# Row-wise weight stages, norm sums inside them, normed rows in PSUM and a later reload of x in a two-block transformer kernel

## The chip, the cores and the metric

The kernel runs on one core of one Trainium2 chip. The metric is the device time of one execution in microseconds (us); the kernel before was timed in three runs.

## What is computed

512 tokens of width 1024 pass through two blocks. In the parts that matter here:

```python
# first block
x = x + gate1 * mixed                      # mixed = (gated branches) @ w_out
h2 = rms_norm(x, g_norm2) * (1 + scale2) + shift2
x = x + gate2 * peer_ffn(h2, w_peer_q, ...)   # top 16 of 128 x 128 experts, 8 heads
# second block, i = 0: windowed attention, i = 1: latent attention
u = rms_norm_2(h, norm_g[i])
y = (attention(u) * silu(z)) @ w_out
h = h + y
gate = sigmoid(rms_norm_2(h, ple_norm_g[i]) @ ple_w_gate[i])
h = h + (p[i] @ ple_w[i]) * gate
# after both
return rms_norm_2(h, final_norm_g)
```

## The kernel before

It is written engine by engine, with its own semaphores; each engine's order is the order of the code. Activations lie transposed: `xT` (the residual) and `hT` (the normed rows) have 8 rows of 128 features by 512 tokens. Every fp32 weight and activation is cut into a high and a low fp16 part, and a product is three fp16 matmuls (`three`, L624). Weights come as tiles of 128x1024 through a ring of four in SBUF (SP, L465); POOL cuts each into parts (L573, L574, L576), also a ring of four: for tile n it waits until PE has begun tile n-3 (semaphore `begun`).

**Stages.** `features` computes one output of 128 features by 512 tokens after another: output m takes the 8 rows k in order, 24 matmuls, and one weight tile. Banks 0 to 3 of PSUM hold the sums in turn; output m waits until output m-4 was taken (`need_bank`), and in output 0 each row k waits for its input (`need(k)`). `ple_w0` and `ple_w1` have two rows, so 6 matmuls an output. `tokens` is the other form: four sums side by side, row by row.

**Norms.** Seven norms (n = 0 to 6) go alike. ACT squares the 8 rows of `xT` into `hT` (L985), PE sums them with a matrix of ones (`norm_part`, L672, an fp32 matmul that the trace shows as two), ACT takes the root (L987), DVE the reciprocal (L1187). Then for each row DVE multiplies (L1190) into `whole`, two rows in SBUF, ACT copies the high part to `hT` (L980, L997), DVE subtracts to get the low part (L1198, L1200) and signals `h_ready`. Stages behind norms: `peer_q` (norm 1), `a_q` (2), `ple_g0` (3), the tokens stage `b_c` (4), `ple_g1` (5); norm 6 gives the output.

**Attention outputs.** PE turns eight blocks into banks 4 to 7; DVE multiplies each with its gate into `whole` (L1578) and cuts it (L1218, L1219); `a_out` and `b_out` read the result. DVE adds their sums to `xT` (L1425).

**Gates.** ACT writes the sigmoid of each `ple_g` output to SBUF (L1133), DVE multiplies (L1594) and adds to `xT` (L1596).

**Experts.** 128 chunks go up (24 matmuls each, into PSUM banks 0 and 1 in turn; ACT's gelu at L1064; SP stores the result, L514); 64 of them have gate matmuls beside them. Four stores of 8 MB take the gates to `gate_mem` (L1095). `xT` was parked in memory before, since its place holds the gates' working rows; it is read back at L1097, right behind the last of these stores on ACT's queue. 64 gates are done by chunk 112; 16 chunks of gelu follow. DVE needs `xT` again at the end of the down phase. Places of the old program that the steps use:

```python
act.dma_start(gate_mem[...], spread[...])            # L1095, four times
act.dma_start(xT[:, :, :], x_park...)                # L1097
gelus(AT_GATES + S // GROUP, CHUNKS)                 # the last 16 chunks
...
norm(1); features("peer_q", hr, h_need(1))           # PE
features("a_out", ...); features("ple_w0", ...)
norm(3); features("ple_g0", hr, h_need(3)); norm(4)
```

## Time and profile before

| | |
|---|---|
| median of 3 runs | 2800.81 us (2798.86 to 2802.94) |
| the profiled execution's own time | 2798.45 us |
| its span | 2796.6 us |
| busy: PE, DVE, ACT, POOL | 2515.2, 1558.5, 594.7, 1602.1 us |
| mean granted TensorE clock | 0.953 of 2.4 GHz |

Busy times are those of instructions; matmuls overlap, so a stage's length is read from starts and from who takes its sums. In a timeline row stand the start and length in us, the engine, line, operation, the tiles, how many instructions, and in brackets the idle time before it with the engine whose work ended it. "ACTq" and "SPq" are DMA issues. Runs of the same kind are merged into one row, whose length reaches from the first start to the last end.

### The profile page before, as it was taken

Reading aid. Unit: us, or ns where it says so; the run is one execution under the profiler, and the core shown is the slowest. Engines: PE = TensorE matmul, PEld = TensorE weight load, DVE = VectorE, ACT = ScalarE, POOL = GpSimd, SP = SyncE. Lnnn points to the kernel's source line nnn. Section 1 sums busy time; section 2 is a strip of 40 time slices with the busy share of each in tenths; the row PEclk is TensorE's granted clock in tenths of the full one; section 3 lists DMA queues with packets and bytes.
Section 4 is the critical chain, followed back from the end, with each engine's and each line's share of the span. In section 5 each row is a group of like instructions: output and inputs, shape, how many; then the busy total and the mean of one; then the engine's idle time right before and its main releaser. Section 6 shows DMA issues by size and latency. Waiting matters only on the chain.

```text
span 2796.6 us, 38708 instructions
## 1 busy us (share of the span) xinstructions
PE 2515.2 (90%) x12856; PEld 1260.3 (45%) x12856; DVE 1558.5 (56%) x2823; ACT 594.7 (21%) x1243; POOL 1602.1 (57%) x1048
## 2 busy tenths in 40 slices
PE   3767788999999999978999999999898888989987
PEld 1423443444455555433444444444355533557633
DVE  6498583699967777505952222250218836555525
ACT  1111221111122222201111111110125322245412
POOL 4535435799976767659976666660560157830053
PEclk7878898999999999989999999999999999999998
DMA  6216312354446587577765555560220022310021
GB/s 228 98 44 215 118 38 80 113 150 143 146 147 199 179 249 246 166 217 254 261 220 204 201 204 201 204 224 15 84 83 1 9 75 68 106 53 1 9 75 38
DMA packets 189252, 375.45 MB, mean 134 GB/s; under 512 B 13536, under 2 KB 79200, under 8 KB 189152
## 3 DMA queue, kind: packets, MB, share of 16 engines
q1 hardware_dynamic: 119696, 332.64, 35.8%
q10 hardware_dynamic: 69456, 41.49, 5.0%
q8 instruction: 61, 1.00, 0.1%
q14 instruction: 39, 0.32, 0.0%
HBM read 302.77 MB, written 71.30 MB: 134 GB/s over the span
## 4 chain that ended last, share of the span: by engine, by line
PE 77%; DVE 12%; DMA 3%; issue 2%; ACT 2%; POOL 2%; ACTq 1%; SPq 0%; DVEq 0%; POOLq 0%
PE ps L624 65%; PE ps L714 3%; PE ps L734 3%; PE ps L840 2%; PE ps L723 2%; DMA arena<-ada_w 2%; DVE arena L1280 2%; PE ps L672 1%; ACTq L1097 1%; DVE arena L1384 1%; DVE arena L1383 1%; DVE spare L1190 1%; DVE arena L1245 1%; ACT arena L1016 1%; DVE arena L1218 1%
## 5 line engine op out<-in xcount | busy, mean ns | idle before, releaser
L624 PE MATMUL ps<-hT,parts 128*128 128x512 f16 x4800 | 1070.3, 383 | 66.1 <-DVE hT L1198 29.6
L573 POOL TENSOR_SCALAR parts<-ring 128x1024 f16<-128x1024 f32 x261 | 297.9, 1141 | 955.3 <-PE ps L624 890.0
L624 PEld LDWEIGHTS ps<-hT,parts 128*128 128x128 f16 x4800 | 466.5, 98 | 642.0 <-issue 43.3
L624 PE MATMUL ps<-arena 128*128 128x512 f16 x3072 | 666.2, 380 | 8.4 <-DVE arena L1544 8.4
L576 POOL TENSOR_TENSOR parts<-ring,parts 128x1024 f16<-128x1024 f32 x261 | 577.2, 2212 | 21.7
L624 PEld LDWEIGHTS ps<-arena 128*128 128x128 f16 x3072 | 300.9, 98 | 374.5 <-issue 15.0
L1539 DVE TENSOR_TENSOR arena<-arena 128x512 f32<-128x512 f32 x128 | 149.7, 1170 | 451.6 <-DMA arena<-gate_mem 447.8
L574 POOL TENSOR_SCALAR ring<-ring 128x1024 f32<-128x1024 f32 x261 | 306.6, 1175 | 0.0
L594 POOL TENSOR_TENSOR arena<-ring,arena 128x1024 f16<-128x1024 f32 x128 | 283.6, 2215 | 10.6
L592 POOL TENSOR_SCALAR arena<-ring 128x1024 f16<-128x1024 f32 x128 | 148.2, 1158 | 169.7 <-PE ps L624 169.7
L624 PE MATMUL ps<-arena,parts 128*128 128x512 f16 x876 | 199.8, 389 | 49.4 <-POOL parts L576 34.3
L1064 ACT ACTIVATE spare<-ps 128x512 f32<-128x512 f32 x128 | 76.4, 597 | 600.3 <-PE ps L624 338.0
L980 ACT ACTIVATE arena<-ps 128x512 f32<-128x512 f32 (+6 forms) x250 | 125.9, 518 | 311.7 <-PE ps L624 309.8
L1103 ACT ACTIVATE arena<-arena 128x512 f16<-128x512 f32 x128 | 80.5, 630 | 522.1 <-DVE arena L1539 522.1
L624 PEld LDWEIGHTS ps<-arena,parts 128*128 128x128 f16 x876 | 86.3, 100 | 162.1 <-POOL parts L576 34.8
L1544 DVE TENSOR_TENSOR arena<-arena 128x512 f16<-128x512 f32 x128 | 123.0, 962 | 5.6 <-ACT arena L1103 5.6
L1515 DVE TENSOR_TENSOR xT<-xT,ps 128x1024 f16<-128x1024 f16 x64 | 78.1, 1221 | 83.7 <-PE ps L840 83.7
L723 PE MATMUL ps<-ident,arena 128*128 128x128 f32 x496 | 87.9, 288 | 24.6 <-ACT arena L1016 23.3
L624 PE MATMUL ps<-parts,hT 128*128 128x512 f16 (+3 forms) x480 | 72.1, 314 | 41.1 <-DVE hT L1200 31.4
L723 PEld LDWEIGHTS ps<-ident,arena 128*128 128x128 f32 x496 | 56.6, 142 | 108.8 <-ACT arena L1016 87.6
L1280 DVE CUSTOM_DVE_ANT_0 arena<-arena,route,vecs 128x1024 f32<-128x1024 f32 x48 | 77.2, 1636 | 29.7 <-DMA arena<-ada_w 29.6
L1242 DVE SCALAR_TENSOR_TENSOR arena<-arena,ps 128x256 f32<-128x256 f32 (+1 forms) x64 | 31.1, 487 | 112.0 <-PE ps L714 110.2
(169 smaller groups left out, 2414.6 us busy)
## 6 DMA issues: line engine op xcount, KB each, us to landing
ring<-w SPq DMA_DIRECT2D x133, 512.0 KB, 3.3
ring<-u SPq DMA_DIRECT2D x128, 512.0 KB, 3.9
ring<-v SPq DMA_DIRECT2D x128, 512.0 KB, 3.4
act_mem<-spare SPq DMA_DIRECT2D x128, 256.0 KB, 4.0
gate_mem<-arena ACTq DMA_DIRECT2D x4, 8192.0 KB, 42.0
arena<-act_mem SPq DMA_DIRECT2D x128, 256.0 KB, 3.6
arena<-gate_mem SPq DMA_DIRECT2D x128, 256.0 KB, 3.8
arena<-ada_w SPq DMA_DIRECT2D x48, 512.0 KB, 4.8
```

Source lines behind the costliest of these rows:

```text
L573: G.tensor_scalar(dst[:, 0, :], src, WS, 1.0, ALU.mult, ALU.mult).then_inc(scaled, 1)
L574: G.tensor_scalar(src, src, WS, 1.0, ALU.mult, ALU.mult).then_inc(scaled, 1)
L576: G.tensor_tensor(dst[:, 1, :], src, dst[:, 0, :], ALU.subtract).then_inc(parts_ready, 1)
L592: G.tensor_scalar(dst[:, 0, :], src, 1.0, 1.0, ALU.mult, ALU.mult).then_inc(v_high, 1)
L594: G.tensor_tensor(dst[:, 1, :], src, dst[:, 0, :], ALU.subtract).then_inc(parts_ready, 1)
L624: ins = [T.matmul(out_, a, b, start=start and j == 0, stop=stop and j == 2) for j, (a, b) in enumerate(((lhs[0], rhs[0]), (lhs[0], rhs[1]) ...
L714: T.matmul(ps[:, 4 + u % 2, 0:rhs.shape[-1]], lhsT, rhs, start=True, stop=True).then_inc(logits, 1)
L723: mm = T.transpose(ps[:, 6 + u % 2, c * P:(c + 1) * P], probs_b[:, u % 2, c * P:(c + 1) * P], ident[:, :])
L980: return A.activation(dst, src, ACT.Copy, scale=scale)
L1280: own.do(V.tensor_tensor_reduce(out=ada_slot(m), in0=ada_slot(m), in1=c_row, scale=1.0, scalar=vecs[:, a:a + 1], op0=ALU.mult, op1=ALU.add ...
L1539: V.tensor_tensor(prod[:, at % 2, :], pair[:, at % 4, 0, :], pair[:, at % 4, 1, :], ALU.mult).then_inc(product, 1)
L1544: V.tensor_tensor(w_parts[:, at, 1, :], prod[:, at % 2, :], w_parts[:, at, 0, :], ALU.subtract).then_inc(weighted, 1)
```

## The change

**A row-wise stage.** `features_wide` replaces `features` for `peer_q`, `a_q`, `a_out`, `ple_g0`, `b_out` and `ple_g1`. For rows 0 to 4 it computes four outputs together: row k of outputs 0, 1, 2, 3, then row k+1. After that it goes on output by output, rows 5 to 7 of the first four, then outputs 4 to 7 whole. So its first row needs four weight tiles. `begun` is counted for tile 0 at the first matmul, and for tiles 1 to 3 only when output m starts its row 5.

**Norm sums.** Parts of norms 1, 3, 4, 5 and 6 stand between outputs. For norm 1 part m-2 follows output m of `out`, two are left behind it. For norms 3 and 5 two follow each of outputs 5, 6 and 7 of `a_out` or `b_out`, the last two follow outputs 1 and 2 of `ple_w`. For norms 4 and 6 two follow each of outputs 5, 6, 7 of `ple_g`, two are left. Squares of norms 4 and 6 go to `aq`, and ACT makes them between the gates. ACT takes the outputs of `ple_w` behind the squares, around the root and between the first copies. A root of one column into `warm` stands before the last square of every norm.

**PSUM.** The reciprocal goes to bank 7, the normed rows to banks 5 and 6, gates too; the gated product to bank 4; the turned block is multiplied in its own bank.

**Reload.** The read of `xT` from `x_park` stands behind the last 16 gelus.

PE from the turned blocks of the second attention to the program's end, before (L706 turns, L624 the three products, L672 norm sums):

```order
L723 MATMUL ps<-ident,arena 128x128 x4
L734 MATMUL ps<-hT,arena 128x64 x8
L706 MATMUL ps<-ident,arena 128x128 x32
L624 MATMUL ps<-arena,parts 128x512 x240
L672 MATMUL ps<-hT,ones 128x512 x8
L624 MATMUL ps<-hT,parts 128x512 x192
L672 MATMUL ps<-hT,ones 128x512 x8
```

and now, the same place up to the start of `ple_g1` (L766 turns, L637 products, L718 norm sums):

```order
L766 MATMUL ps<-ident,arena 128x128 x32
L637 MATMUL ps<-arena,parts 128x512 x144
L718 MATMUL ps<-hT,ones 128x512 x2
L637 MATMUL ps<-arena,parts 128x512 x24
L718 MATMUL ps<-hT,ones 128x512 x2
L637 MATMUL ps<-arena,parts 128x512 x24
L718 MATMUL ps<-hT,ones 128x512 x2
L637 MATMUL ps<-arena,parts 128x512 x12
L718 MATMUL ps<-hT,ones 128x512
L637 MATMUL ps<-arena,parts 128x512 x6
L718 MATMUL ps<-hT,ones 128x512
L637 MATMUL ps<-arena,parts 128x512 x30
```

The eight sums of norm 5 moved from behind `ple_w1` to between its outputs and those of `b_out`; 30 products (five outputs) stand behind the last of them.

ACT at the end of the gates, before (L1070 gates, L1064 gelu):

```order
L1070 ACTIVATE arena<-ps 128x128x4
L1090 REGISTER_ALU
L1090 COMPARE_AND_BRANCH
L1095 DMA gate_mem<-arena 128x128x128
L1097 DMA xT<-x_park 128x8x512
L1075 UNCONDITIONAL_BRANCH
```

and now (L1134 gelu, L1173 the down phase's first work):

```order
L1134 ACTIVATE spare<-ps 128x512
L1145 REGISTER_ALU
L1145 COMPARE_AND_BRANCH
L1168 DMA xT<-x_park 128x8x512
L1175 UNCONDITIONAL_BRANCH
L1175 ISA
L1173 ACTIVATE arena<-arena 128x512
```

The reload has moved past the loop with the last 16 gelus and stands ahead of the down phase's copies.

The diff, its lines of context cut:

```diff
--- before
+++ after
@@ -158,6 +158,7 @@
         eps = sb("eps", [P, 1])
+        warm = sb("warm", [P, 8])
         spare = sb("spare", [P, 1536])
@@ -262,7 +263,6 @@
         soft_w = cut(2, S)
-        gate_t, prod_t = probs_w, soft_w
         small_w = cut(80)
@@ -364,6 +364,19 @@
+        whole_root = ps[:, 7, :]
+        def normed_row(k):
+            return ps[:, 5 + k % 2, :]
+        def gate_row(m):
+            return ps[:, 5 + m % 2, :]
+        gated_row = ps[:, 4, :]
+        def squares_of(n):
+            return aq if n in (4, 6) else hT
         def count_taken(name, i):
@@ -629,7 +642,7 @@
-            def features(name, rhs, need=None):
+            def features(name, rhs, need=None, after=None):
                 st = stages[name]
@@ -645,6 +658,39 @@
                     last.then_inc(summed, 1)
+                    if after is not None:
+                        after(m)
+            def features_wide(name, rhs, need, after=None):
+                st = stages[name]
+                early, side = 5, 4
+                def unit(m, k):
+                    return three(bank(st.s0 + m), piece(st.t0 + m, k * P, P), rhs(k), k == 0, k == KC - 1)
+                for k in range(early):
+                    need(k)
+                    for m in range(side):
+                        if k == 0:
+                            need_bank(st.s0 + m)
+                            need_tile(st.t0 + m)
+                        first, last = unit(m, k)
+                        if k == m == 0:
+                            first.then_inc(begun, 1)
+                for m in range(st.outs):
+                    if m >= side:
+                        need_bank(st.s0 + m)
+                        need_tile(st.t0 + m)
+                    for k in range(early if m < side else 0, KC):
+                        if m == 0:
+                            need(k)
+                        first, last = unit(m, k)
+                        if m > 0 and k == (early if m < side else 0):
+                            first.then_inc(begun, 1)
+                    last.then_inc(summed, 1)
+                    if after is not None:
+                        after(m)
@@ -669,13 +715,27 @@
                 pe.wait_ge(squares, KC * n + k + 1)
-                mm = T.matmul(norm_bank(n), ones[:, :], hT[:, k, :], start=(k == 0), stop=(k == KC - 1))
+                mm = T.matmul(norm_bank(n), ones[:, :], squares_of(n)[:, k, :], start=(k == 0), stop=(k == KC - 1))
                 if k == KC - 1:
...
                 for k in range(KC):
+                    norm_part(n, k)
+            def behind(n, lag):
+                return lambda m: norm_part(n, m - lag) if lag <= m < KC + lag else None
+            def late_pairs(n):
+                def after(m):
+                    for k in range(2 * (m - 5), 2 * (m - 5) + 2):
+                        if m >= 5:
+                            norm_part(n, k)
+                return after
+            def last_parts(n, lag):
+                for k in range(KC - lag, KC):
                     norm_part(n, k)
@@ -791,9 +851,9 @@
             features("up_attn", in_parts(oT), lambda k: pe.wait_ge(turned_read, 6 + k + 1))
-            features("out", in_parts(gT), lambda k: pe.wait_ge(tok_ready, 3 + k + 1))
-            norm(1)
-            features("peer_q", hr, h_need(1))
+            features("out", in_parts(gT), lambda k: pe.wait_ge(tok_ready, 3 + k + 1), behind(1, 2))
+            last_parts(1, 2)
+            features_wide("peer_q", hr, h_need(1))
             st = stages["subkeys"]
@@ -900,7 +960,7 @@
                 norm_part(2, k)
-            features("a_q", hr, h_need(2))
+            features_wide("a_q", hr, h_need(2))
             features("a_k", hr)
@@ -911,13 +971,11 @@
                 turn([(i, a_tok[:, i, b * P:(b + 1) * P]) for i in range(NT)])
-            features("a_out", in_parts(az), lambda k: pe.wait_ge(turned_read, t_a + k + 1))
-            features("ple_w0", in_parts(pT), lambda k: pe.wait_ge(p_ready, k + 1))
-            norm(3)
-            features("ple_g0", hr, h_need(3))
-            norm(4)
+            features_wide("a_out", in_parts(az), lambda k: pe.wait_ge(turned_read, t_a + k + 1), late_pairs(3))
+            features("ple_w0", in_parts(pT), lambda k: pe.wait_ge(p_ready, k + 1),
+                     lambda m: norm_part(3, KC - 3 + m) if m in (1, 2) else None)
+            features_wide("ple_g0", hr, h_need(3), late_pairs(4))
+            last_parts(4, 2)
             tokens("b_c", hl, h_need(4))
@@ -958,11 +1016,11 @@
                 turn([(i, btok[:, i, b * P:(b + 1) * P]) for i in range(NT)])
-            features("b_out", in_parts(bz), lambda k: pe.wait_ge(turned_read, t_o + k + 1))
-            features("ple_w1", in_parts(pT), lambda k: pe.wait_ge(p_ready, 2 + k + 1))
-            norm(5)
-            features("ple_g1", hr, h_need(5))
-            norm(6)
+            features_wide("b_out", in_parts(bz), lambda k: pe.wait_ge(turned_read, t_o + k + 1), late_pairs(5))
+            features("ple_w1", in_parts(pT), lambda k: pe.wait_ge(p_ready, 2 + k + 1),
+                     lambda m: norm_part(5, KC - 3 + m) if m in (1, 2) else None)
+            features_wide("ple_g1", hr, h_need(5), late_pairs(6))
+            last_parts(6, 2)
@@ -979,18 +1037,30 @@
-            def norm(n, need, shift_of=None):
-                for k in range(KC):
-                    need(k)
-                    own.do(A.activation(hT[:, k, :], xT[:, k, :], ACT.Square), squares)
+            def square(n, k, need):
+                if k == KC - 1:
+                    own.do(A.activation(warm[:, n:n + 1], eps[:, 0:1], ACT.Sqrt))
+                need(k)
+                own.do(A.activation(squares_of(n)[:, k, :], xT[:, k, :], ACT.Square), squares)
+            def norm(n, need=None, shift_of=None, between=None):
+                if need is not None:
+                    for k in range(KC):
+                        square(n, k, need)
+                if between is not None:
+                    between(-2)
                 act.wait_ge(norm_sum, n + 1)
...
                     return
+                if between is not None:
+                    between(-1)
                 for k in range(KC):
+                    if between is not None:
+                        between(k)
                     act.wait_ge(norm_whole, KC * n + k + 1)
                     hi, _ = halves(hT[:, k, :])
-                    src = whole[:, k % 2, :]
+                    src = normed_row(k)
                     if shift_of is None:
@@ -1094,8 +1164,8 @@
                               spread[:, b % 2, :, :]).then_inc(gates_out[b % 2], 16)
+            gelus(AT_GATES + S // GROUP, CHUNKS)
             act.dma_start(xT[:, :, :], x_park.rearrange("c p n -> p c n")).then_inc(x_back, 16)
-            gelus(AT_GATES + S // GROUP, CHUNKS)
@@ -1122,19 +1192,30 @@
             attention(units_window(), U_WINDOW)
-            take("ple_w0", lambda s, b: copy(ple[:, s, :], b))
             def ple_gate(name, n):
-                norm(n, x_from("a_out" if n == 3 else "b_out"))
+                def embedded(k):
+                    first, last = {-2: (0, 3), -1: (3, 6), 1: (6, 7), 2: (7, 8)}.get(k, (0, 0))
+                    take("ple_w0" if n == 3 else "ple_w1", lambda s, b: copy(ple[:, s, :], b), first, last)
+                norm(n, x_from("a_out" if n == 3 else "b_out"), between=embedded)
...
                         act.wait_ge(sig_used, (0 if name == "ple_g0" else KC) + s - 1)
-                    return A.activation(gate_t[:, s % 2, :], b, ACT.Sigmoid, scale=1.0 / WS)
-                take(name, gate)
+                    return A.activation(gate_row(s), b, ACT.Sigmoid, scale=1.0 / WS)
+                def of_sum(k):
+                    act.wait_ge(x_ready, (0 if name == "ple_g0" else KC) + k + 1)
+                for s in range(KC + 1):
+                    if s < KC:
+                        take(name, gate, s, s + 1)
+                    if s >= 1:
+                        square(n + 1, s - 1, of_sum)
             ple_gate("ple_g0", 3)
-            norm(4, lambda k: act.wait_ge(x_ready, k + 1))
+            norm(4)
             take("b_c", lambda s, b: copy(lat[:, s, 0:512], b))
@@ -1161,9 +1242,8 @@
             act.wait_ge(turned_read, 14 + KC + 5 + 2 * B_H + KC)
-            take("ple_w1", lambda s, b: copy(ple[:, s, :], b))
             ple_gate("ple_g1", 5)
-            norm(6, lambda k: act.wait_ge(x_ready, KC + k + 1))
+            norm(6)
             for k in range(0, KC, 2):
@@ -1184,16 +1264,16 @@
                 dve.wait_ge(norm_root, n + 1)
-                own.link(V.reciprocal(root, root))
+                own.link(V.reciprocal(whole_root, root))
                 def normed(k, dst, signal):
-                    own.do(V.scalar_tensor_tensor(out=dst, in0=xT[:, k, :], scalar=g_of(k), in1=root,
+                    own.do(V.scalar_tensor_tensor(out=dst, in0=xT[:, k, :], scalar=g_of(k), in1=whole_root,
                                                   op0=ALU.mult, op1=ALU.mult), signal)
...
                     dve.wait_ge(h_high, KC * n + k + 1)
-                    src = whole[:, k % 2, :]
+                    src = normed_row(k)
                     if shift_of is None:
@@ -1208,7 +1288,7 @@
                     if k < KC:
-                        normed(k, whole[:, k % 2, :], norm_whole)
+                        normed(k, normed_row(k), norm_whole)
                     if k >= 1:
@@ -1575,8 +1655,8 @@
                     src = ps[:, 4 + (turned_n[0] - 1) % 4, :]
-                    own.link(V.tensor_tensor(whole[:, b % 2, :], src, z[:, b, :], ALU.mult))
-                    cut_block(halves(z[:, b, :]), whole[:, b % 2, :], signal=turned_read)
+                    own.link(V.tensor_tensor(src, src, z[:, b, :], ALU.mult))
+                    cut_block(halves(z[:, b, :]), src, signal=turned_read)
@@ -1591,9 +1671,9 @@
                     own.settle()
-                    own.do(V.tensor_tensor(prod_t[:, m % 2, :], gate_t[:, m % 2, :], ple[:, m, :], ALU.mult), sig_used)
+                    own.do(V.tensor_tensor(gated_row, gate_row(m), ple[:, m, :], ALU.mult), sig_used)
                     own.settle()
-                    own.do(V.tensor_tensor(xT[:, m, :], xT[:, m, :], prod_t[:, m % 2, :], ALU.add), x_ready)
+                    own.do(V.tensor_tensor(xT[:, m, :], xT[:, m, :], gated_row, ALU.add), x_ready)
...
             add_ple("ple_g0", 0)
```

## Rows read from the trace of the kernel before

**Rows 1.** The page's part 4: the chain that ended last, by engine.

```profile
PE 77%; DVE 12%; DMA 3%; issue 2%; ACT 2%; POOL 2%; ACTq 1%; SPq 0%; DVEq 0%; POOLq 0%
```

**Rows 2.** Timeline, PE's last gate chunk, ACT's reload of x, PE's next chunk.

```profile
1174.66 10.52 PE L624 MATMUL ps<-hT,parts 128*128 128x512 f16 x48
1176.06 30.77 ACTq L1097 DMA_DIRECT2D xT<-x_park  x1
1207.75 74.61 PE L624 MATMUL ps<-hT,parts 128*128 128x512 f16 x336 [22.56 <-ACT spare L1064]
```

**Rows 3.** DMA view: issues by size, median us to landing; first two 1170 to 1220 us.

```profile
act_mem<-spare SPq DMA_DIRECT2D x4, 256.0 KB, 7.0
xT<-x_park ACTq DMA_DIRECT2D x1, 2048.0 KB, 42.8
...
x_park<-xT ACTq DMA_DIRECT2D x1, 2048.0 KB, 9.1
```

**Rows 4.** Window behind that stall: stretch, length, PE busy, PEclk, DMA share, GB/s.

```profile
1210.00:1212.00 2.00, 2.00 (x7) 0.58 0.88 228
```

**Rows 5.** Timeline, norm 1 and the first rows of peer_q.

```profile
458.57 7.03 PE L672 MATMUL ps<-hT,ones 128*128 128x512 f32 x16
...
472.19 2.82 PE L624 MATMUL ps<-hT,parts 128*128 128x512 f16 x6 [6.58 <-DVE hT L1200]
472.97 1.43 POOL L573 TENSOR_SCALAR parts<-ring 128x1024 f16<-128x1024 f32 x1 [14.73 <-PE ps L624]
476.41 2.49 DVE L1190 SCALAR_TENSOR_TENSOR spare<-xT,gain,spare 128x512 f32<-128x512 f32 x1
479.62 42.38 PE L624 MATMUL ps<-hT,parts 128*128 128x512 f16 x183 [1.73 <-DVE hT L1200]
```

**Rows 6.** Timeline, POOL cuts one weight tile first and last of its three instructions.

```profile
486.16 1.05 POOL L573 TENSOR_SCALAR parts<-ring 128x1024 f16<-128x1024 f32 x1 [7.80 <-PE ps L624]
...
488.30 2.13 POOL L576 TENSOR_TENSOR parts<-ring,parts 128x1024 f16<-128x1024 f32 x1
```

**Rows 7.** Timeline, first rows of a_q and the take of its last output.

```profile
1969.62 2.76 PE L624 MATMUL ps<-hT,parts 128*128 128x512 f16 x6 [6.53 <-DVE hT L1198]
...
2019.82 0.60 ACT L980 ACTIVATE arena<-ps 128x512 f32<-128x512 f32 x1 [4.58 <-PE ps L624]
```

**Rows 8.** Timeline, end of a_out, norm 3, start and end of ple_g0, norm 4.

```profile
2268.21 0.69 DVE L1425 SCALAR_TENSOR_TENSOR xT<-ps,xT 128x512 f32<-128x512 f32 x1 [4.49 <-PE ps L624]
...
2279.74 7.13 PE L672 MATMUL ps<-hT,ones 128*128 128x512 f32 x16 [1.21 <-ACT hT L985]
...
2293.31 2.76 PE L624 MATMUL ps<-hT,parts 128*128 128x512 f16 x6 [6.43 <-DVE hT L1198]
...
2342.69 0.60 ACT L1133 ACTIVATE arena<-ps 128x512 f32<-128x512 f32 x1 [4.58 <-PE ps L624]
2344.04 0.69 DVE L1596 TENSOR_TENSOR xT<-xT,arena 128x512 f32<-128x512 f32 x1
2347.45 1.28 ACT L987 ACT_TABLE_LOAD   x1
2351.03 0.69 ACT L987 ACTIVATE spare<-ps,eps 128x512 f32<-128x512 f32 x1 [2.29 <-PE ps L672]
```

**Rows 9.** Timeline, turned blocks of attention and the start of a_out.

```profile
2215.17 0.43 DVE L1218 TENSOR_SCALAR arena<-spare 128x512 f16<-128x512 f32 x1
...
2222.66 5.42 PE L624 MATMUL ps<-arena,parts 128*128 128x512 f16 x18
2226.17 0.68 DVE L1578 TENSOR_TENSOR spare<-ps,arena 128x512 f32<-128x512 f32 x1
```

**Rows 10.** Timeline, b_out: first matmuls, take of the last output.

```profile
2653.66 4.96 PE L624 MATMUL ps<-arena,parts 128*128 128x512 f16 x18
...
2700.89 0.69 DVE L1425 SCALAR_TENSOR_TENSOR xT<-ps,xT 128x512 f32<-128x512 f32 x1 [4.49 <-PE ps L624]
```

**Rows 11.** Timeline, up_attn: three matmuls after a gap.

```profile
415.16 0.82 PE L624 MATMUL ps<-arena,parts 128*128 128x512 f16 x3 [2.90 <-DVE arena L1219]
```

## The prediction

> **What bounds the kernel now.** I read the chain that ended last first. It gives PE 77% and DVE 12% [rows 1], so work taken off other engines counts only where PE waits for it. The timelines of PE at the changed places come next. Three kinds of stall stand there.
>
> First, PE waits 22.56 us for a gelu of ACT, while ACT stands 30.77 us in the issue of the reload of x, behind its own 8 MB store of gates [rows 2]. Behind the stall the granted clock is 0.50, then 1.00, which are 1.2 and 2.4 GHz; the window from 1210 to 1212 shows 0.58 [rows 4], a rise in its last sixth, 4 us after PE's start at 1207.75.
>
> Second, a norm. `a_out` ends at 2268.1 (its last sum is taken at 2268.21). `ple_w0` follows, PE waits 1.21 us for a square, sums for 7.13, waits 6.43 for root, reciprocal and the first row, and starts `ple_g0` at 2293.31 [rows 8]: 25.2 us in all.
>
> Third, output 0 of a stage behind a norm. Its eight rows come at DVE's pace, and one DVE multiply takes 2.49 us while POOL cuts a tile [rows 5]. An output at full rate takes 5.18 us (0.60 and 4.58 between two takes [rows 7]), eight 41.4. `peer_q` took from 472.19 to 522.0, 49.8 us [rows 5]; `a_q` 50.1 [rows 7]; `ple_g0` 49.3 (to its last take at 2342.69) [rows 8], and `ple_g1` repeats it within 0.1. Behind attentions `a_out` took 45.5 [rows 8, 9] and `b_out` 47.2 [rows 10], which has the cuts of the embeddings in DVE's way.
>
> **Reload.** Removed are the 22.56 us of idle time and the half clock behind it: 336 matmuls took 74.61 us, 14 outputs' worth at 5.18 is 72.5, so 2.1 [rows 2, 7]: 24.6. In its new place ACT has nothing waiting in front of the down phase but this issue. A store of the same 2 MB landed in 9.1 us, and not 42.8, with the queue free [rows 3]; DVE wants x only at the end of the down phase, 600 us later. New is that PE now runs while the last gate store fills the DMA engines. ACT's gelu must wait for SP's store of two chunks ago, and such stores then take 7.0 us [rows 3]. SP issues one, as I estimate from its order (a weight load that waits for POOL stands ahead), one chunk of 5.18 us behind its gelu; 5.18 and 7.0 are 12.2 where two chunks are 10.4, so a gelu comes some 2 us late. PE wants it only 5.18 us after its sum, so with its own 0.6 some 2 us are left. The lower bound is no stall, the upper 4 us. I take **-23.8** (-24.6 to -20).
>
> **The row-wise start.** With four outputs at once PE spends 2.59 us on a row at full rate. DVE makes one in about 1.4: each of its two operations per row now has an operand in PSUM, and such operations took 0.68 and 0.69, the first in the middle of POOL's work [rows 8, 9], where one between SBUF rows took 2.49 [rows 5]. So PE never waits for a row but the first. It waits for the fourth tile instead: POOL may cut it only when the first is begun. At `peer_q` POOL started 0.78 us after PE [rows 5]. From the first to the end of the last of its instructions, alone, are 4.27 us [rows 6]. With the signals, output 3 can start 5.2 us after the stage. PE has three units of three matmuls before that (3.8 us at 1.2 GHz, 1.9 at 2.4), then the other 61 units at 0.648, 39.5 us. A wide stage takes **44.7 us**, or 44.5 where PE comes from work and signals sooner, if the clock is full from then on. The upper bound of the cut is the contended one, 5.3: 1 us more a stage.
>
> Later tiles: the fifth may be cut when output 1 starts its row 5, unit 24, 17.9 us after the start; it is there at 22.9 and wanted at unit 32, 23.8. The next have more room. No term, but only 0.9 us of cover.
>
> So `peer_q` gains **5.1**, `a_q` **5.4**, `ple_g0` and `ple_g1` **4.9** each, 9.8. At the attentions DVE's cut now reads PSUM: 0.69 for 0.43 [rows 9], the same shape. Four rows stand before the first product, so the stage starts 1.05 us later. `a_out`: 45.5 against 45.8, **+0.3**. `b_out`: 47.2 against 45.8, **-1.4**.
>
> **The clock.** A wide stage behind an idle PE starts at 1.2 GHz, and its tile wait comes just where the clock would rise. If it doesn't rise before the wait, some 4 us more run at half rate, 2 us lost. Between 0 and 2 for each of the four stages of this kind, I take 1. Before `ple_g0` and `ple_g1` PE is busy, and a gap of 3.1 us follows 1.9 us of work. Behind a gap of 2.90 three matmuls still took 0.82 us, the full rate [rows 11]; behind 6.58, six took 2.82 with one short wait, the low one [rows 5]. I take 0.7 each, with the same bounds. Sum **+5.4** (0 to 12).
>
> [...]
>
> **Norms 3 and 5.** The eight sums cost PE 0.86 us each wherever they stand (7.03 for eight, [rows 5]). Now four stand before the end of `a_out` (3.4 us). Behind it come two sums (1.7), three outputs of `ple_w` (3.9) with two sums (1.7), and the last five outputs (6.5): 13.8. Root, reciprocal and first row need 6.4 after the last sum, and the five outputs (1.30 each, a quarter of 5.18) hide them. The square is long there; ACT's three takes end before the root, and output 7 needs take 3, which is 3 us early. Before 25.2, now 17.2: **-8.0** each, less 0.1 for signals, -15.8. If the cover is gone, the first row is late next, by what ACT's takes push it.
>
> **Norms 1, 4, 6.** After the end of `ple_g0` the root started 8.4 us later (2342.6 to 2351.03) [rows 8]. Now the last square waits for a table load of 1.28 [rows 8] behind square 6: gate 0.8, square 6 to 1.4, load and warm root to 3.0, square to 3.6, sum to 4.5, and 3.4 before the end. 7.9 against 8.4: **-0.4** each for 4 and 6; -0.2 for norm 1, where five sums stand before the end and the last waits until 1.8 us after it. Norms 0 and 2 gain nothing: their table load was hidden behind sums.
>
> **Sum.** -23.8 -5.1 -5.4 -9.8 +0.3 -1.4 -15.8 -1.0 +5.4 = -56.6. From 2798.45, the profiled execution, that is 2741.9; the median of the runs is 2.4 above it, so **2744 us**. Bounds: all clock and stall terms at their best, 2738, with 3 for what a row taken once may be off, 2735. At worst +6.6 (clock), +3.8 (stores), +6 (contended cuts): 2760, and 2 more for scatter, 2762.
>
> **Rivals.**
> - *The clock drops at every tile wait.* For it: PE's 1.9 to 3.8 us of work ahead is less than the 4 us after which it rose [rows 4]. Against: the three matmuls behind 2.90. +6.6: 2751. Chance 0.15.
> - *The reload keeps ACT.* If the 30.77 us were the reload's own and not its queue's, ACT would stand there when the down phase wants its first copy: 24 us come back, 2768. Against: its place behind 8 MB, 9.1 us for the twin. 0.05.
> - *The reload meets the loads of v and of the first pairs* at the turn to the down phase, where PE waits anyway and where the weights come through a ring of four: 2 MB take 9.1 us [rows 3]. At most all of it is added, and I price it at half, 4.5: 2749. 0.06.
> - *PSUM operands don't free DVE from POOL.* Rows of 2.49 us still fit in 2.59, so only the tile comes later: +6, 2750. 0.05.
> - *Slower than before.* The clock stays at 1.2 GHz far into every wide stage, since weights rotate through four banks between waits. Each microsecond of it costs half; six stages must lose 57 us, so it decides from 19 us of low clock a stage. A whole stage at 1.2 GHz would give about 2980. Against: it rose 4 us after PE's start [rows 4], and `peer_q`'s last 183 matmuls, 39.5 us at full rate, took 42.38 [rows 5]: low for 6. 0.02.
> - *The forecast*, 2744: 0.67.
>
> The forecast, the first rival, the third and the fourth lie in **2735 to 2762**, 0.93; I leave it so for terms that I can't see, such as the order in which signals arrive. A measurement of this kernel can tell about 0.2% (6 us) from no change. All but the slower case and a remnant are faster by far more: faster 0.97, same 0.01, slower 0.02.
>
> **What the profile after would show.** No PE wait at the end of the gates, and the reload's issue under 1 us. In each wide stage three units, one wait for POOL's L576 of 1 to 3.5 us, and none after it; 44 to 47 us a stage. DVE's multiply at 0.75 or less throughout the norms, and 0.69 for each turned cut. No wait of more than 1 us between the end of `a_out` and `ple_g0`, and PEclk at 1.00 there. One wait of about 1 us before the last sum of norms 4 and 6. It is wrong if PE waits for tiles after the fourth, if gelus fall behind during the gate store, or if ACT's takes push the first row of norms 3 and 5.

## The result, and the profile after

The changed kernel takes 2738.35 us (median of 4 runs, 2737.59 to 2741.39); the kernel before, timed beside it, 2799.89. The ratio is 0.978, with a 95% interval of 0.9764 to 0.9797: 61.5 us less. The profiled execution has a span of 2736.4 us, 60.2 less than before, and a mean granted clock of 0.962.

The chain that ended last, by engine. DVE is down a point against [rows 1], and POOL, which was 2%, is now 3%: the wait for the fourth tile.

```profile
PE 78%; DVE 11%; POOL 3%; DMA 3%; issue 2%; ACT 2%; SPq 0%; DVEq 0%; POOLq 0%; ACTq 0%
```

**The reload.** Timeline of after at the end of the gates. It answers to [rows 2].

```profile
1170.44 83.04 PE L637 MATMUL ps<-hT,parts 128*128 128x512 f16 x384
...
1184.19 0.60 ACT L1134 ACTIVATE spare<-ps 128x512 f32<-128x512 f32 x1 [7.69 <-DMA act_mem<-spare]
...
1253.66 0.38 ACTq L1168 DMA_DIRECT2D xT<-x_park  x1
```

The last 16 chunks are one unbroken row of 384 matmuls, 83.04 us; before, they took 107.7, from 1174.66 to 1282.36. ACT's gelus now do wait for stores, but never so long that PE notices. The issue of the reload takes 0.38 us and not 30.77, and the transfer lands in 10.5.

**The row-wise stage.** Timeline of after at `peer_q`, its PE, POOL and DVE rows; they answer to [rows 5].

```profile
472.94 3.43 PE L637 MATMUL ps<-hT,parts 128*128 128x512 f16 x9 [6.47 <-DVE hT L1280]
478.16 39.66 PE L637 MATMUL ps<-hT,parts 128*128 128x512 f16 x183 [1.79 <-POOL parts L589]
```

```profile
473.75 1.05 POOL L586 TENSOR_SCALAR parts<-ring 128x1024 f16<-128x1024 f32 x1 [10.41 <-PE ps L637]
474.76 1.05 POOL L587 TENSOR_SCALAR ring<-ring 128x1024 f32<-128x1024 f32 x1
475.89 2.12 POOL L589 TENSOR_TENSOR parts<-ring,parts 128x1024 f16<-128x1024 f32 x1
```

```profile
475.81 0.76 DVE L1270 SCALAR_TENSOR_TENSOR ps<-xT,gain,ps 128x512 f32<-128x512 f32 x1
```

Three units (nine matmuls), one wait for POOL's cut, then 183 matmuls without a gap. The wait ends 5.2 us after the start. The windows from the start of `peer_q` (length, PE busy, PEclk, DMA share, GB/s) show that the clock rose before the wait, some 2.7 us after PE's start, and stayed up behind it:

```profile
472.94:474.94 2.00, 2.00 (x5) 0.50 0.00 0
474.94:476.94 2.00, 1.43 (x5) 0.83 0.00 0
476.94:478.94 2.00, 0.78 (x4) 1.00 0.00 0
478.94:480.94 2.00, 2.00 (x11) 1.00 0.77 262
```

A multiply beside POOL's cut takes 0.76 us where it took 2.49, and POOL's instructions keep their own length.

**Norm 3 and `ple_g0`.** Timeline of after, PE only; it answers to [rows 8].

```profile
2237.95 1.88 PE L718 MATMUL ps<-hT,ones 128*128 128x512 f32 x4
...
2245.26 6.64 PE L637 MATMUL ps<-arena,parts 128*128 128x512 f16 x30
2251.75 2.12 PE L637 MATMUL ps<-hT,parts 128*128 128x512 f16 x9
2256.74 30.98 PE L637 MATMUL ps<-hT,parts 128*128 128x512 f16 x135 [2.88 <-POOL parts L589]
...
2301.36 2.74 PE L718 MATMUL ps<-arena,ones 128*128 128x512 f32 x6
2304.76 1.12 PE L718 MATMUL ps<-arena,ones 128*128 128x512 f32 x2 [0.67 <-ACT arena L1044]
2312.30 22.41 PE L637 MATMUL ps<-parts,hT 128*128 128x512 f16 x96 [6.41 <-DVE hT L1278]
```

`a_out` ends at 2237.95, `ple_g0` starts 13.80 us later and without a wait. Then the clock: the 135 matmuls behind the tile wait take 30.98 us, and the same 135 in `ple_g1` take 29.30.

```profile
2670.76 2.12 PE L637 MATMUL ps<-hT,parts 128*128 128x512 f16 x9
2675.75 29.30 PE L637 MATMUL ps<-hT,parts 128*128 128x512 f16 x135 [2.88 <-POOL parts L589]
```

Windows of 2 us behind the wait of `ple_g0`, with the same columns. PEclk falls to 0.50, 1.2 GHz, and comes back within 4 us of the first of these windows; in `ple_g1` every such window shows 1.00.

```profile
2257.75:2259.75 2.00, 2.00 (x6) 0.50 0.70 260
2259.75:2261.75 2.00, 2.00 (x8) 0.74 0.00 0
2261.75:2263.75 2.00, 2.00 (x11) 1.00 0.00 0
```

### The profile page after: what moved, and what is told of

Same layout as the page of the kernel before. It is cut to its first block, busy times and chain, and to the rows that moved or that the text cites. A ratio compares the mean times of both kernels' runs of the same rounds, so it can differ in the third digit from the quotient of the medians.

```text
span 2736.4 us, 38715 instructions
## 1 busy us (share of the span) xinstructions
PE 2500.3 (91%) x12856; PEld 1263.7 (46%) x12856; DVE 1522.5 (56%) x2823; ACT 596.5 (22%) x1250; POOL 1584.0 (58%) x1048
## 4 chain that ended last, share of the span: by engine, by line
PE 78%; DVE 11%; POOL 3%; DMA 3%; issue 2%; ACT 2%; SPq 0%; DVEq 0%; POOLq 0%; ACTq 0%
PE ps L637 66%; PE ps L774 3%; PE ps L794 3%; DMA arena<-ada_w 2%; PE ps L900 2%; PE ps L783 2%; DVE arena L1360 2%; PE ps L718 1%; DVE arena L1464 1%; DVE arena L1463 1%; POOL ring L587 1%; DVE arena L1325 1%; ACT arena L1086 1%; DVE arena L1299 1%; POOL parts L589 1%
## 5 line engine op out<-in xcount | busy, mean ns | idle before, releaser
L637 PE MATMUL ps<-hT,parts 128*128 128x512 f16 x4800 | 1056.4, 381 | 26.0 <-POOL parts L589 9.1
L637 PEld LDWEIGHTS ps<-hT,parts 128*128 128x128 f16 x4800 | 467.6, 98 | 586.7 <-issue 24.4
L637 PE MATMUL ps<-arena 128*128 128x512 f16 x3072 | 667.5, 380 | 6.7 <-DVE arena L1624 6.7
L589 POOL TENSOR_TENSOR parts<-ring,parts 128x1024 f16<-128x1024 f32 x261 | 571.1, 2188 | 21.8
L637 PEld LDWEIGHTS ps<-arena 128*128 128x128 f16 x3072 | 301.3, 98 | 373.8 <-issue 14.9
L587 POOL TENSOR_SCALAR ring<-ring 128x1024 f32<-128x1024 f32 x261 | 298.4, 1143 | 0.0
L637 PE MATMUL ps<-arena,parts 128*128 128x512 f16 x876 | 202.5, 390 | 46.6 <-POOL parts L589 37.4
L1134 ACT ACTIVATE spare<-ps 128x512 f32<-128x512 f32 x128 | 76.5, 597 | 575.2 <-PE ps L637 309.3
L1173 ACT ACTIVATE arena<-arena 128x512 f16<-128x512 f32 x128 | 80.6, 630 | 521.3 <-DVE arena L1619 521.1
L637 PEld LDWEIGHTS ps<-arena,parts 128*128 128x128 f16 x876 | 86.6, 100 | 164.3 <-POOL parts L589 34.8
L783 PE MATMUL ps<-ident,arena 128*128 128x128 f32 x496 | 88.0, 288 | 25.5 <-ACT arena L1086 24.7
L637 PE MATMUL ps<-parts,hT 128*128 128x512 f16 (+3 forms) x480 | 70.6, 310 | 41.7 <-DVE hT L1280 32.0
```

The lines of the kernel that those rows point to most:

```text
L587: G.tensor_scalar(src, src, WS, 1.0, ALU.mult, ALU.mult).then_inc(scaled, 1)
L589: G.tensor_tensor(dst[:, 1, :], src, dst[:, 0, :], ALU.subtract).then_inc(parts_ready, 1)
L637: ins = [T.matmul(out_, a, b, start=start and j == 0, stop=stop and j == 2) for j, (a, b) in enumerate(((lhs[0], rhs[0]), (lhs[0], rhs[1]) ...
L783: mm = T.transpose(ps[:, 6 + u % 2, c * P:(c + 1) * P], probs_b[:, u % 2, c * P:(c + 1) * P], ident[:, :])
```

## The experiments

A stage's length below runs from its first matmul to the next work of PE, less the norm sums inside it (3.44 us); that of `peer_q` runs to the first matmul of `subkeys`.

The kernels were timed in three groups, each with the kernel before beside it: 2803.31 us with the reload alone, one output after another, the rows in SBUF and the sums behind; 2802.57 with the reload four gelus behind, three and two side by side and the turned product in SBUF; 2800.12 with the rest. Beside after it took 2799.89. So a difference to after given in us can be off by some 3 us; the ratios allow for that. One execution of each kernel was profiled.

### The reload alone

The kernel before, with this edit; all others start from after.

```diff
-            act.dma_start(xT[:, :, :], x_park...)
             gelus(AT_GATES + S // GROUP, CHUNKS)
+            act.dma_start(xT[:, :, :], x_park...)
```

> The kernel before with one edit: the reload of x stands behind the last 16 gelus. Theory (the stall is the queue's, and all of it goes): the trace of after shows the last chunks' 384 matmuls in 83.0 us where before they took 107.7, so 24.7 less: about 2775 us. Rival 1 (a good part of the gain at this place came from other edits, or the reload makes a new stall at the turn to the down phase): 2785 or more. Rival 2 (the issue of 30.8 us is the reload's own): 2798 or more, with an issue of some 30 us in front of the down phase.

Measured: 2777.27 us against 2803.31 beside it, ratio 0.9909 (0.9893 to 0.9926), 26.0 us less. The theory holds. The place itself takes 24.7 us less, as in after, so the term is this edit's alone. (The two traces' spans differ by 21.8 only: this one came 1.8 us late to the place and lost 1.0 more behind it.)

```profile
1176.50 83.04 PE L624 MATMUL ps<-hT,parts 128*128 128x512 f16 x384
```

### The reload four gelus behind the store

```diff
-            gelus(AT_GATES + S // GROUP, CHUNKS)
+            gelus(AT_GATES + S // GROUP, AT_GATES + S // GROUP + 4)
             act.dma_start(xT[:, :, :], x_park...)
+            gelus(AT_GATES + S // GROUP + 4, CHUNKS)
```

> The kernel after with the reload of x behind the first 4 of the last 16 gelus, in place of behind all 16, so that it is issued some 16 to 21 us after the last store of gates. Theory (ACT stands in the issue until the store of gates ahead of it on the same queue is nearly through, which lands 43.6 us after its issue and let the reload go 30.8 after): a stall of 10 to 15 us of ACT, of which PE can bridge one chunk, so 2743 to 2752 us. Rival 1 (the issue's length is the reload's own): 30 us of stall, 2760 or more. Rival 2 (only a reload right behind the store stalls): 2738.

Measured: 2760.37 us (2758.68 to 2761.14), the number of the first rival, but not by its mechanism. Timeline, ACT's issue and PE:

```profile
1201.42 15.61 ACTq L1168 DMA_DIRECT2D xT<-x_park  x1
```

```profile
1177.71 31.24 PE L637 MATMUL ps<-hT,parts 128*128 128x512 f16 x144
1217.95 54.92 PE L637 MATMUL ps<-hT,parts 128*128 128x512 f16 x240 [9.00 <-ACT spare L1134]
```

The issue takes 15.61 us: not the 30 of an own cost, and not nothing. Issued right behind the store it took 30.77, 22.7 us later 15.61, and with the queue free 0.38. It ended 2.8 us before the store landed in before (34.0 us after the store's issue) and 2.4 us before it landed here (40.7 us), so its length follows the store ahead on the queue. PE loses 12.1 us here (95.16 for the 384 matmuls and the wait, against 83.04). Another 7.3 had been lost ahead of it, in code that this edit doesn't touch: 3.3 in `peer_q` and `subkeys`, which ran partly at 1.2 GHz (below), 2.9 in the expert stage for a reason that is open, and 1.1 before `peer_q`. The median alone would have given the wrong verdict.

### One output after another, rows in PSUM

```diff
-            features_wide("peer_q", hr, h_need(1))
+            features("peer_q", hr, h_need(1))
```

The five other stages alike.

> The kernel after with all six stages in the old order, output by output; rows in PSUM and norm sums stay as they are. Theory (order and PSUM rows each do a part): DVE's rows come every 1.4 us, so output 0 takes some 11 us, of which 5.2 is work, and the stage some 47 to 47.5 behind a norm against 44.5 to 46; at the attentions 44.5, no change. Four stages by 2.5 is +10: about 2748 us. Rival (only the order counts, PSUM rows do nothing): the stages go back to 49.3 to 50.1, +20: 2758 or more. Second rival (only the PSUM rows count): 2738 to 2741.

Measured: 2743.78 us (2742.98 to 2745.83), 0.979 of before (0.9774 to 0.9807). That is 5.4 above after, half of what I expected, and the intervals overlap. In the traces the six stages together take 3.0 us more: `peer_q`, `a_q` and `ple_g1` 1.6, 1.2 and 1.4 more, `a_out`, `b_out` and `ple_g0` 0.5, 0.5 and 0.3 less. In `ple_g1` each of the first rows has a short wait, at full rate:

```profile
2678.94 0.82 PE L637 MATMUL ps<-hT,parts 128*128 128x512 f16 x3 [0.56 <-DVE hT L1278]
2680.32 0.82 PE L637 MATMUL ps<-hT,parts 128*128 128x512 f16 x3 [0.56 <-DVE hT L1278]
```

### The row-wise order with the rows in SBUF

```diff
-        whole_root = ps[:, 7, :]
+        whole_root = root
-            return ps[:, 5 + k % 2, :]
+            return whole[:, k % 2, :]
```

> The kernel after with the normed rows and the reciprocal back in SBUF; order of the stages as in after. Theory (the row-wise order hides a row of 2.5 us, only POOL's cut of the fourth tile is later, by about 1 us in each of four or five stages): 2742 to 2743 us, DVE multiplies of up to 2.5 us beside POOL's cuts and no PE wait for a row but the first two. Rival (DVE and POOL together fall behind 2.59 us a row, so PE waits for rows too): 2750 or more. Second rival (PSUM operands change nothing that PE waits for): 2738.

Measured: 2756.31 us (2753.83 to 2758.64), 18.0 above after; the traces' spans differ by 16.2. My expectation falls; the size is the rival's, though PE waits for no row but the first. The timeline at `peer_q`:

```profile
474.82 1.47 POOL L587 TENSOR_SCALAR ring<-ring 128x1024 f32<-128x1024 f32 x1
...
476.38 2.44 POOL L589 TENSOR_TENSOR parts<-ring,parts 128x1024 f16<-128x1024 f32 x1
476.87 2.49 DVE L1270 SCALAR_TENSOR_TENSOR spare<-xT,gain,spare 128x512 f32<-128x512 f32 x1
478.96 13.29 PE L637 MATMUL ps<-hT,parts 128*128 128x512 f16 x53 [2.50 <-POOL parts L589]
```

Both engines are held up: POOL's three instructions take 5.5 us together, not 4.3, so the tile is late, as I had said. What I had left out comes behind it. The granted clock is down behind the wait in all four norm stages and in `b_out`, longest in `ple_g1`, whose 135 matmuls take 32.11 us for 29.30. And the first row of `ple_g0` and `ple_g1` is 1.50 us late:

```profile
2255.14 3.04 DVE L1270 SCALAR_TENSOR_TENSOR spare<-xT,vecs,spare 128x512 f32<-128x512 f32 x2
...
2258.97 2.12 PE L637 MATMUL ps<-hT,parts 128*128 128x512 f16 x9 [1.50 <-DVE hT L1278]
```

By stages this is +2.9, +2.8, +0.7, +1.5 and +3.6 (`peer_q`, `a_q`, `ple_g0`, `b_out`, `ple_g1`), twice +1.7 ahead of `ple_g0` and `ple_g1`, and +1.4 in `b_c`: all of the 16.2. Sorted by cause, the later tile makes 3.8 of it (1.2, 1.1, 0.75 and 0.75 in the four norm stages), the two late first rows 3.3, and the clock 9.1. The first two are this edit's. Whether the 9.1 are is not shown, since the clock of these stages also differs between kernels that have the same rows (below).

The Trainium skill (SBUF — State Buffer, section on the two separate sides) states that a DVE operation with two SBUF inputs and a GpSimd operation that reads SBUF exclude each other from a shared port pair for a whole instruction. The trace agrees: beside POOL's cut the multiply takes up to 2.49 us with both operands in SBUF (0.75 with POOL idle) and 0.76 with one in PSUM, and POOL is slower only in the first case.

### The sums of norms 3 and 5 behind `ple_w`

```diff
-            features_wide("a_out", ..., late_pairs(3))
-            features("ple_w0", ..., lambda m: norm_part(3, KC - 3 + m) if m in (1, 2) else None)
+            features_wide("a_out", ...)
+            features("ple_w0", ...)
+            norm(3)
```

Norm 5 alike; ACT takes all of `ple_w` ahead of the root.

> The kernel after with the sums of norms 3 and 5 all behind ple_w, and ACT's takes of ple_w all ahead of the root; the rest as in after. Theory (root, reciprocal and first row, some 6.5 us, are hidden by the five outputs of ple_w that stand behind the last sum): +6.5 twice, less the 1.7 us that ple_g0 loses by its start now: about 2750 to 2752 us, with a PE wait of 6.4 us before ple_g0 and ple_g1. Rival (what counts is the wide stage's start, which waits for the fourth tile either way): 2741 or less.

Measured: 2755.33 us (2755.05 to 2756.27), 17.0 above after. The wait is there, and from the start of `a_out` to that of `ple_g0` are 68.45 us for 61.97, +6.5 as expected, and +6.5 again in the second block. `ple_g0` itself is 1.5 us shorter and `ple_g1` 0.2 longer, so the edit makes 11.7:

```profile
2250.27 7.03 PE L718 MATMUL ps<-hT,ones 128*128 128x512 f32 x16
2263.62 4.02 PE L637 MATMUL ps<-hT,parts 128*128 128x512 f16 x9 [6.32 <-DVE hT L1278]
```

The rest lies mostly ahead of the edit, 3.3 us of it at the `peer_q` stage and the next:

```profile
478.76 41.62 PE L637 MATMUL ps<-hT,parts 128*128 128x512 f16 x183 [1.19 <-POOL parts L589]
521.93 9.32 PE L637 MATMUL ps<-parts,arena 64*128 64x128 f16 x192 [1.55 <-issue]
```

In after these are 39.66 and 7.81 us. The windows behind the tile wait (PEld, DVE, ACT and POOL stand between PE busy and PEclk) show the low clock for 4 us, and the one before them, in the wait, shows it too. So the clock did not fall behind the wait here; it had not risen before it:

```profile
477.55:478.55 1.00, 0.02 (x1) 0.50 0.00 0
```

```profile
478.76:480.76 2.00, 2.00 (x5) 0.69 (x6) 1.93 (x4) 1.24 (x2) 0.00 (x0) 0.50 0.55 162
480.76:482.76 2.00, 2.00 (x6) 0.73 (x5) 1.90 (x3) 0.71 (x2) 0.00 (x0) 0.50 0.25 100
```

### Three and two outputs side by side

```diff
-                early, side = 5, 4
+                early, side = 5, 3
```

and `5, 2`.

> The kernel after with three outputs side by side in place of four, so that the first row needs three tiles, which are all cut. Theory (in after PE waits 1.4 to 2.9 us a stage for POOL's fourth tile, and nothing else ends later): the wait goes at all six starts, 4 by 1.5 and 2 by 2.9, and the 1.7 us of clock at ple_g0: 12 to 13 less, about 2726 us. A row is 1.94 us of PE and DVE makes one in 1.45. Rival (the fourth tile is now wanted early as well, or the clock is lower without the wait): 2735 to 2738.

> The kernel after with two outputs side by side. Theory: PE spends 1.30 us on a row and DVE makes one in 1.45, so PE waits a little for each of some six rows, 1 us a stage, and never for a tile: 2727 to 2732 us. Rival (short waits at each row keep the granted clock low for longer, or DVE's rows are slower than 1.45 beside POOL's cuts): 2735 or more.

Measured: three side by side 2725.63 us (2722.61 to 2727.73), 0.9727 of before (0.9714 to 0.974), so 12.7 below after; two 2728.62 (2728.35 to 2733.07). Both as expected. With three no wait is left in any of the six stages:

```profile
473.54 44.52 PE L637 MATMUL ps<-hT,parts 128*128 128x512 f16 x192 [6.47 <-DVE hT L1280]
```

```profile
2247.18 31.25 PE L637 MATMUL ps<-hT,parts 128*128 128x512 f16 x144
```

`ple_g0` takes 41.4 us and not 46.2, full rate throughout. `peer_q` gains only 0.35: 192 matmuls at full rate are 41.4 and it takes 44.52, since behind an idle PE the first 6 us run at 1.2 GHz, where in after only the first 2.7 did. That is the clock's doing and not the order's: in the next kernel, with the same three-wide `peer_q`, the low stretch is 3.6 us and the stage takes 44.9.

| us | before | order alone (rows in SBUF) | PSUM rows alone | both: after | three side by side | two |
|---|---|---|---|---|---|---|
| `peer_q` | 51.4 | 49.3 | 48.1 | 46.4 | 46.1 | 44.9 |
| `ple_g1` | 49.3 | 48.0 | 45.9 | 44.5 | 41.4 | 42.7 |

The PSUM rows alone give more than half of the gain. The order adds to it, and loses part of that to the tile which it asks for too early. The Trainium skill (TensorE: Matmul & The Clock Gate, HAM oscillation in real kernels) advises for thin M (under 512), where PE waits for a DMA between K-tiles: "restructure the loop K-contiguous (do all K-tiles for one M-tile before DMA-waiting) so PE stays warm". That is not this case, whose matmuls are 512 wide and whose waits are for DVE and POOL. Here the order that finishes one output first is the column of the PSUM rows alone, and the row-wise order without a tile wait beats it by 4.4 us in `ple_g1`; the trace shows no loss of clock in either.

### The turned product in SBUF again

```diff
-                    own.link(V.tensor_tensor(src, src, z[:, b, :], ALU.mult))
-                    cut_block(halves(z[:, b, :]), src, signal=turned_read)
+                    own.link(V.tensor_tensor(whole[:, b % 2, :], src, z[:, b, :], ALU.mult))
+                    cut_block(halves(z[:, b, :]), whole[:, b % 2, :], signal=turned_read)
```

(on top of three side by side)

> The three-wide kernel, and the turned block is multiplied with its gate into SBUF again, as before, so that DVE's cut takes 0.43 and not 0.69 us. Theory (the first product of a_out and b_out stands behind four such cuts; it started 1.09 us later in after): 1.1 us less twice, about 2724 us. Rival (with the product in SBUF DVE shares its port with POOL, or the turned blocks are held by another engine): the same as the three-wide kernel.

Measured: 2725.31 us, no difference from the three-wide kernel that runs can tell. In the trace `a_out` and `b_out` do start 1.1 us sooner, but they last 0.4 and 1.0 longer. In `b_out` the windows show the clock rising later; whether the earlier start is the reason is not shown.

### A PE kept busy

```diff
+            def busy(name):
+                st = stages[name]
+                need_tile(st.t0)
+                hi, lo = piece(st.t0, 0, P)[0], piece(st.t0, 0, 512)[1]
+                for j in range(26):
+                    T.matmul(ps[:, 4, :], hi, lo, start=True, stop=True)
...
+            busy("peer_q")
             features_wide("peer_q", hr, h_need(1))
```

The same ahead of `a_q` and `b_c`; the extra products go to a bank that nobody reads.

> The three-wide kernel, and in front of peer_q, a_q and b_c PE multiplies the first weight tile with itself 26 times into a bank that nobody reads, while it would wait 6.3 to 6.5 us for root, reciprocal and first row: extra work of 5.6 us at full rate, and no result changes. Theory (a stage behind an idle PE starts at 1.2 GHz; in the three-wide kernel that cost 3.0 us at peer_q, 1.7 at a_q and up to 3 at b_c, over 192, 240 and 96 matmuls at 0.216 each): all of it goes, up to 7.8 us: 2718 to 2720 us, PEclk 1.00 from the first matmul. Rival (the low clock comes whatever PE did before, or the products delay the first row's matmuls): 2725 or more.

> The same 26 idle-time products in the kernel that has three outputs side by side and the turned product in SBUF. Theory (its two turns are 1.08 us shorter each; of that 0.4 and 1.0 came back as low clock in a_out and b_out, which these products don't touch): as the kernel with the products alone, or 1 us less, 2717 to 2720 us. Rival (with the clock kept up the two gains add fully): 2716 or less.

> The kernel after with the same 26 products ahead of peer_q, a_q and b_c. Theory (in after the low clock at peer_q and a_q lies within the 5.2 us for which output 3 waits for its tile anyway, so it costs nothing there): the wait for POOL grows from 1.8 and 1.5 to about 3.1 us and the two stages keep their length; only b_c gains, 1.5 us: 2736.5 to 2738. Rival (the clock term of the forecast is real and paid in these stages): 4 us or more less, 2734 or less.

The first, three-wide: 2725.49 us (2721.27 to 2725.96), no less than without the products, so the rival's number. Yet the trace shows the clock gain at each place. `peer_q` has 192 matmuls in 41.61 us for 44.52, and `b_c` 20.88 for 23.83 (43.38 and 22.36 in the kernel with the turned product in SBUF, which has no such products either, so part of this is the clock's own variation):

```profile
471.95 41.61 PE L637 MATMUL ps<-hT,parts 128*128 128x512 f16 x192 [0.86 <-DVE hT L1290]
```

```profile
2300.80 20.88 PE L637 MATMUL ps<-parts,hT 128*128 128x512 f16 x96 [0.80 <-DVE hT L1288]
```

Between them 2.1 us were lost again in the expert stage. The profiled execution is the fastest of its five and that of the three-wide kernel the slowest, so the two spans (2719.5 and 2725.9) overstate what the medians deny. Whether the products are worth anything in this kernel stays open.

The second, with the turned product in SBUF too: 2720.92 us (2720.62 to 2724.56), 0.9718 of before (0.9704 to 0.9731). It is the lowest median, 17.4 below after, whose interval it doesn't touch. That is just above the theory's 2717 to 2720, and the rival's 2716 or less fails. From the three-wide kernel it can't be told safely.

The third, four-wide as after: 2743.97 us (2741.35 to 2747.4), 5.6 above after, though its interval (0.9786 to 0.9816) overlaps that of after, and the traces' spans differ by 3.1. Theory and rival both miss. The wait for POOL grew to 2.88 us, as expected. `b_c` gains 1.5 us, as expected, but now the clock falls behind the tile wait at `peer_q` and at `ple_g1`, and no longer at `ple_g0`:

```profile
478.90 41.34 PE L637 MATMUL ps<-hT,parts 128*128 128x512 f16 x183 [2.88 <-POOL parts L589]
```

```profile
2677.24 30.98 PE L637 MATMUL ps<-hT,parts 128*128 128x512 f16 x135 [2.87 <-POOL parts L589]
```

### A later start of `peer_q`

```diff
                 act.wait_ge(norm_sum, n + 1)
+                if n == 1:
+                    for _ in range(3):
+                        own.link(A.activation(warm[:, 7:8], eps[:, 0:1], ACT.Sqrt))
```

> The kernel after with three one-column roots on ACT ahead of the root of norm 1, which start peer_q some 0.6 to 0.9 us later and change nothing else. Theory (whether the clock falls again behind the tile wait depends on when the stage starts, and in after it was luck that it didn't: two other kernels of this study with the same stage took 58.4 us from the start of peer_q to that of the expert stage and not 55.3): either 0.7 us more in all, 2739, or some 3 to 6 more, 2742 to 2745, if the new start falls badly; the trace then shows PEclk under 1 behind the tile wait. Rival (the length of the stage doesn't depend on its start): 55.3 us again, and the extra time of the two other kernels comes from what they changed.

Measured: 2744.75 us (2743.78 to 2748.39), 6.4 above after for 0.8 us of added work. That is in the theory's second range. The intervals of the ratios overlap, the runs themselves don't.

```profile
475.02 4.02 PE L637 MATMUL ps<-hT,parts 128*128 128x512 f16 x9 [7.26 <-DVE hT L1283]
480.23 41.23 PE L637 MATMUL ps<-hT,parts 128*128 128x512 f16 x183 [1.19 <-POOL parts L589]
523.01 9.31 PE L637 MATMUL ps<-parts,arena 64*128 64x128 f16 x192 [1.55 <-issue]
```

```profile
480.23:482.23 2.00, 2.00 (x5) 0.50 0.49 156
```

From `peer_q` to the expert stage are 58.2 us, near the 58.6 of the kernels with the sums behind and with the reload four gelus behind, and 55.3 in after, so the rival fails. In all three the granted clock is 0.50 behind the tile wait (the window above), and the nine matmuls ahead of it take 4.02 us, all at 1.2 GHz, where after has 3.43. The same code of a stage gives another clock in another program. That its start decides is likely but not shown: the start was 2.1 us later, of which the edit explains 0.8, and the other two kernels start only 0.6 and 1.1 us later than after. Of the 7.4 us between the spans 2.1 lie ahead of `peer_q`, 2.9 in it and `subkeys`, 1.1 in the expert stage and some 1 in the down phase.

## Why the prediction was right, and where not

| step of the prediction | forecast | in the profile |
|---|---|---|
| reload, stall and half clock | -23.8 | -24.7 |
| `peer_q`, `a_q` | -5.1, -5.4 | -4.9, -5.3 |
| `ple_g0`, `ple_g1` | -4.9, -4.9 | -3.2, -4.9 |
| `a_out`, `b_out` | +0.3, -1.4 | +0.3, -1.4 |
| the clock | +5.4 | 1.7 of it, in `ple_g0`'s -3.2 |
| norms 3 and 5 | -15.8 | -15.9 |
| norms 1, 4, 6 | -0.2, -0.4, -0.4 | +0.4, -0.4, -0.1 |
| `b_c`, not in the sum | 0 | -0.7, its clock |

The right column sums to -60.8; the spans differ by 60.2. Without the clock the forecast is -62.0 and the profile, without the 1.7 and the 0.7 of `b_c`, -61.8, so the sum was right as a mechanism and its clock term too large for this kernel.

**Reload.** The whole stall and its half clock went, as the kernel with that edit alone shows. The caution of 0.8 us for the gelus behind the stores wasn't needed: the longest wait, 7.69 us, was still covered. The rivals at the turn to the down phase fell: from the end of the last gelu chunks to PE's second stretch are 24.1 us before and after.

**The wide stage.** Three units, a wait until 5.2 us after the start, then no gap: as forecast, 44.9 us at `peer_q` and `a_q` and 44.5 in `ple_g1` for my 44.7 and 44.5. The stage's gain is not mainly the order's, though. One step on which I was wrong is the price of a rival, "PSUM operands don't free DVE from POOL": I said they did, which holds, and priced the other case at +6, all of it a later tile. With the rows in SBUF the later tile cost 3.8 us. The late first rows, which I had put at nothing, cost 3.3, and 9.1 of low clock came on top, whose cause is open.

**The clock** was the mis-sized step: "between 0 and 2 for each", taken as 1 four times and 0.7 twice. After paid 1.7 in `ple_g0` and nothing in the five others. The experiments show that the term varies between programs in which the stage's code is the same; a mean of 1 says little about one of them. For `peer_q` the condition of the prediction, "if it doesn't rise before the wait", explains most cases: in after the clock rose before the wait, and nothing was lost. In three kernels with the same stage (sums behind, reload four gelus behind, later start) it didn't, and they lost 2.0, 2.0 and 1.6 us there, and 1.5 more in `subkeys`. In two others, with PE kept busy and with the rows in SBUF, it was up before the wait and fell behind it, 1.7 us each. Behind the wait of 2.88 us that follows a busy PE it fell in five of ten cases in four kernels. So the first rival, "the clock drops at every tile wait", was never wholly true and never wholly false, and after did well by luck.

My argument against that rival rested on a single row, which doesn't repeat. [rows 11] has three matmuls at full rate behind a gap of 2.90 us. The same three in after, behind the same gap, ran at 1.2 GHz:

```profile
415.55 1.46 PE L637 MATMUL ps<-arena,parts 128*128 128x512 f16 x3 [2.90 <-DVE arena L1299]
```

Of the 14 kernels traced, eight took 0.82 us at this place, two 0.91 and 1.03, and four 1.46.

**Norms.** The 13.80 us behind `a_out` are the 13.8 of the working. At norm 1 I forecast -0.2 and found +0.4, which is not the norm's: the 171 matmuls of `out` ahead of it take 38.8 us without the sums, against 38.4, and from the end of `out`, sums moved inside it included, `peer_q` starts 0.1 sooner.

## What to carry over

When a loop order is changed to hide late rows, count what its first row needs of every other resource: one side-by-side output fewer took away a tile wait at six starts and 12.7 us. A DMA issue placed behind a large store on the same queue blocks the engine that issues it, so put it behind the work that others wait for. And compare stage by stage: the kernels with the reload four gelus behind and with the rows in SBUF both had the median of a rival whose mechanism the trace doesn't show, since 7.3 us of the one lay ahead of the edit and 9.1 of the other in the clock.

## What I had not expected of the hardware

The cost of an idle gap isn't a property of the gap. The same wait of 2.87 or 2.88 us, behind a busy PE, was followed by a full clock in five places and by 1.2 GHz in five, at 1.7 us each, in stages whose code is the same. When the wait comes is the likely reason, but no run moved only that. How much it varies between executions of one program is not shown either, as each has one trace; the runs of the kernel with the sums behind lie within 1.2 us, those of the four-wide kernel with a busy PE within 6.1. So an edit far away can look like a gain or loss of 3 to 6 us, as much as lies between the runs of one program. From its start to the last 16 chunks the expert stage took 642.1 to 642.3 us in most kernels, and 643.2 to 645.2 in others. Why is open, and wasn't tried.
